# Sample states spread over forty branch products, head norms moved among the swish gate products

## What is computed

```python
u_x, u_y, q, k, v, g, mq, gates = split(rmsnorm(x) @ w_in)
a_out = (h * gelu(u_y)) @ w_branch_lru                 # recurrent branch
# retention, 4 heads; for a sample: s = s * decay + k v ; o = q s   (s0 from state_ret, s is an output)
o, s_new = retention(rotary(q), rotary(k), v, s_prev)
o = o * rsqrt(mean(o * o, per head) + EPS)             # head norm
b_out = (silu(g) * o) @ w_branch_ret                   # swish gate, then 2048 x 1024
c_out = attention(mq, mem_k, mem_v) @ w_branch_mem
merged = sigmoid(g_a) * a_out + sigmoid(g_b) * b_out + sigmoid(g_c) * c_out
x = x + merged @ w_out
x = x + moe(rmsnorm(x))                                # 32 experts of 3 x 2 MB, top 2 of a group
```

## Time and profile before

| | |
|---|---|
| median of 3 runs | 1172.71 us (1172.45 to 1174.39) |
| the profiled execution's own time | 1173.44 us |
| its span, first to last instruction | 1171.6 us |
| TensorE / its weight loads busy | 961.7 us (82%) / 705.9 us (60%) |
| VectorE / ScalarE / GpSimd busy | 366.6 / 221.4 / 100.9 us |
| granted TensorE clock, mean | 0.952 |
| moved by DMA | 343.8 MB, mean 293 GB/s |

### The profile page before, as it was taken

How to read it: one execution, slowest core, us unless ns; L and a number is a source line. 1 busy time by engine, 2 the same in 40 slices (tenths; PEclk the granted TensorE clock), 3 DMA queues, 4 the chain that set the end, 5 groups by cost and what they waited for, 6 DMA issues and landing times.

```text
span 1171.6 us, 16329 instructions
## 1 busy us (share of the span) xinstructions
PE 961.7 (82%) x6950; PEld 705.9 (60%) x6950; DVE 366.6 (31%) x681; ACT 221.4 (19%) x453; POOL 100.9 (9%) x122
## 2 busy tenths in 40 slices
PE   7999999999999888999999888566647667675655
PEld 6888888768876666788888645333324333333323
DVE  3303573376223224452111362111162111111113
ACT  2112124114331222241000142010101011010102
POOL 0001121000123332100000140000000000000000
PEclk9999999999999999999999999998988888889897
DMA  9874466694569799745347949999999999999991
GB/s 318 277 251 153 158 216 229 191 278 124 201 231 307 245 299 317 255 144 181 108 144 274 372 167 416 417 417 417 417 417 415 418 416 417 415 418 416 416 404 62
DMA packets 138825, 343.80 MB, mean 293 GB/s; under 512 B 7640, under 2 KB 91864, under 8 KB 122360
## 3 DMA queue, kind: packets, MB, share of 16 engines
q1 hardware_dynamic: 124288, 290.05, 65.7%
q0 software_dynamic: 14464, 52.68, 13.3%
HBM read 320.48 MB, written 22.20 MB: 292 GB/s over the span
## 4 chain that ended last, share of the span: by engine, by line
PE 47%; SPq 22%; DMA 20%; DVE 5%; issue 4%; ACT 2%; POOL 1%; DVEq 0%; ACTq 0%; POOLq 0%
PE psum L961 28%; SPq L783 22%; DMA out_ret_s<-arena 10%; DMA arena<-in_w_up 8%; PE psum L693 3%; PE psum L1015 3%; PE psum L970 2%; PE psum L1027 2%; PE psum L703 2%; PE psum L677 1%; ACT arena L1301 1%; DVE arena L1664 1%; DMA arena<-arena 1%; POOL arena L866 1%; DMA arena<-in_state_ret 1%
## 5 line engine op out<-in xcount | busy, mean ns | idle before, releaser
L961 PE MATMUL psum<-arena 128*128 128x264 f32 x2048 | 473.6, 388 | 0.0
L961 PEld LDWEIGHTS psum<-arena 128*128 128x128 f32 x2048 | 387.6, 191 | 76.3 <-issue 12.0
L693 PE MATMUL psum<-arena 128*32 128x256 f32 x2048 | 148.4, 440 | 119.0 <-DMA arena<-in_w_up 118.1
L693 PEld LDWEIGHTS psum<-arena 128*32 128x32 f32 x2048 | 79.0, 123 | 181.8 <-issue 158.0
L1301 ACT ACTIVATE arena<-psum 128x264 f32<-128x264 f32 (+5 forms) x160 | 67.5, 439 | 350.8 <-PE psum L961 269.0
L1965 DVE SCALAR_TENSOR_TENSOR arena<-arena,psum 128x128 f32<-128x128 f32 x32 | 9.2, 288 | 237.0 <-ACT arena L1510 237.0
L1301 ACT ACTIVATE arena<-arena 128x1024 f32<-128x1024 f32 (+7 forms) x67 | 58.7, 903 | 106.7 <-DVE arena L1819 84.8
L703 PE MATMUL psum<-arena 128*32 128x256 f32 x1024 | 66.4, 402 | 11.8 <-ACT arena L1522 11.7
L1772 DVE SCALAR_TENSOR_TENSOR arena<-arena 128x512 f32<-128x512 f32 x64 | 45.6, 774 | 82.0 <-ACT arena L1301 81.9
L1229 PE MATMUL psum<-arena 128*128 128x264 f32 x112 | 40.1, 441 | 24.1 <-DVE arena L1977 24.1
L703 PEld LDWEIGHTS psum<-arena 128*32 128x32 f32 x1024 | 31.2, 115 | 41.3 <-ACT arena L1522 21.9
(11 more groups left out here) (246 smaller groups left out, 738.1 us busy)
## 6 DMA issues: line engine op xcount, KB each, us to landing
arena<-in_w_gate SPq DMA_DIRECT2D x64, 1024.0 KB, 22.8
arena<-in_w_up SPq DMA_DIRECT2D x64, 1024.0 KB, 22.5
arena<-in_w_down SPq DMA_DIRECT2D x64, 1024.0 KB, 22.9
arena<-in_w_in SPq DMA_DIRECT2D x48, 1024.0 KB, 5.4
arena<-in_state_ret POOLq DMA_DIRECT2D x16, 1024.0 KB, 7.1
out_ret_s<-arena POOLq DMA_DIRECT2D x16, 1024.0 KB, 9.3
arena<-in_w_mem_kv SPq DMA_DIRECT2D x8, 1024.0 KB, 11.6
arena<-in_cache_mem_k POOLq DMA_DIRECT2D x8, 1024.0 KB, 5.6
```

The source lines that it names most:

```text
L693: mm = pe.matmul(psum[32 * a:32 * a + SLOTS, bank, 0:256], tokens[:, 4 * half + k, SLOTS * j:SLOTS * (j + 1)], w[:, :, k, P * a:P * (a + 1 ...
L961: mm = pe.matmul(ps(task)[:, 0:T], w[:, k, (i % 2) * P:(i % 2 + 1) * P], rhs[:, k, :], start=k == 0, stop=k == KT - 1 and not two)
```

## The change

The eight gb products join the branch products, so that the head products and the sixteen half states are woven over forty products instead of thirty-two. The head norms no longer stand among the gb products but among the first seven g products: soT directly behind gb7, oq0 before g0, oq1 and on0 before g1, oq2 and on1 before g2, oq3 and on2 before g4, on3 before g6. VectorE's part of a g task becomes a task of its own, ("gev", i), one g product later in the list, and it uses no PSUM bank of its own. The lifetimes of the buffers follow: what lived to "gc" now lives to "gb", and the norms' scratch lies in stage "g".

```diff
 BUFFERS = {
-    "dmask": (NMASK, "load", "gc"),
+    "dmask": (NMASK, "load", "gb"),
...
-    "st": (3 * 4 * DV, "rows", "gc"),
+    "st": (3 * 4 * DV, "rows", "gb"),
...
-    "os": (DV, "ga", "gb"),
+    "os": (DV, "ga", "g"),
...
-    "sq2": (2 * 4 * T, "gb", "gb"),
+    "sq2": (2 * 4 * T, "g", "g"),
...
-    branches = t("ga", 8) + t("lru_out", 8) + t("gc", 8) + t("mem_out", 8)
+    branches = t("ga", 8) + t("lru_out", 8) + t("gc", 8) + t("mem_out", 8) + t("gb", 8)
     middle = weave(branches, ret[1:])
-    onorm = [("soT",), ("oq", 0), ("oq", 1), ("on", 0), ("oq", 2), ("on", 1), ("oq", 3), ("on", 2), ("on", 3)]
+    norms = {0: [("oq", 0)], 1: [("oq", 1), ("on", 0)], 2: [("oq", 2), ("on", 1)], 4: [("oq", 3), ("on", 2)],
+             6: [("on", 3)]}
+    gated = [("soT",)]
+    for i in range(VT):
+        gated += norms.get(i, []) + [("g", i)] + ([("gev", i - 1)] if i else [])
+    gated += [("gev", VT - 1)]
...
-        + weave(t("gb", 8), onorm) + t("g", 16) + t("ret_out", 8) + t("x2", 8) + [("x2_sq",)]
+        + gated + t("ret_out", 8) + t("x2", 8) + [("x2_sq",)]
...
-                elif kind == "g":
+                elif kind == "gev":
                     i = task[1]
                     dve.wait_ge(g_tanh, i + 1)
                     x = gt[:, i % 2, :]
-                    v(V.scalar_tensor_tensor(x, x, 1.0, ps(task)[:, 0:T], ALU.add, ALU.mult), free_of(task))
+                    v(V.scalar_tensor_tensor(x, x, 1.0, ps(("g", i))[:, 0:T], ALU.add, ALU.mult), free_of(("g", i)))
                     v(V.tensor_tensor(oT[:, i, :], oT[:, i, :], x, ALU.mult), ret_ready)
```

More of the change, by code:

```diff
@@ L154 @@
     "conv_st": (KT * 16, "ux", "x2"),
-    "qT": (KT * T, "q", "gc"),
-    "kT": (KT * T, "k", "gc"),
+    "qT": (KT * T, "q", "gb"),
+    "kT": (KT * T, "k", "gb"),
     "rtmp": (HEADS * 2 * T, "k", "v"),
     "vT": (VT * T, "v", "rows"),
-    "vs_rows": (HEADS * DV, "rows", "gc"),
-    "vb": (2 * D, "rows", "gc"),
-    "st": (3 * 4 * DV, "rows", "gc"),
+    "vs_rows": (HEADS * DV, "rows", "gb"),
+    "vb": (2 * D, "rows", "gb"),
+    "st": (3 * 4 * DV, "rows", "gb"),
     "p32": (TP, "k", "k"),
@@ L164 @@
     "cs": (TP, "k", "rows"),
-    "QM": (KT * 2 * NS * NS, "k", "gc"),
+    "QM": (KT * 2 * NS * NS, "k", "gb"),
     "pqk": (KT * NS, "k", "rows"),
     "qkb": (HEADS * NS, "rows", "rows"),
-    "vqk": (VT * NS, "rows", "gb"),
-    "attT": (2 * 384, "rows", "gc"),
+    "vqk": (VT * NS, "rows", "g"),
+    "attT": (2 * 384, "rows", "gb"),
     "oT": (VT * T, "ga", "ret"),
-    "os": (DV, "ga", "gb"),
+    "os": (DV, "ga", "g"),
     "merged": (KT * T, "ga", "x2"),
@@ L306, in tensor_order @@
         + middle[:4] + weave(middle[4:], so)
-        + weave(t("gb", 8), onorm) + t("g", 16) + t("ret_out", 8) + t("x2", 8) + [("x2_sq",)]
+        + gated + t("ret_out", 8) + t("x2", 8) + [("x2_sq",)]
     )
-NO_PSUM = {"oq", "xq", "lam", "sd", "conv", "kl", "lru", "lru_root", "gelu", "gelu_tanh", "rot_q", "rot_k"}
+NO_PSUM = {"oq", "gev", "xq", "lam", "sd", "conv", "kl", "lru", "lru_root", "gelu", "gelu_tanh", "rot_q", "rot_k"}
 PROJECTIONS = {"mk", "mv", "mq", "ux", "uy", "q", "k", "v", "g", "ga", "gb", "gc", "lru_out", "ret_out",
```

## The result

The changed kernel takes 1165.4 us (median of 5, 1163.6 to 1166.75) against 1172.45 us (5 runs, 1171.4 to 1174.39): a ratio of 0.9938, 95% interval 0.9923 to 0.9952, so 7 us or 0.6% faster. The forecast was 1162.7 us, 10 us faster, with a range of 1152.5 to 1170.5. The sign, the mechanism and the range held; nearly a third of the forecast gain was missing.

What follows compares the result with a forecast made beforehand. Bound: neither TensorE nor DMA full in the state stage, then TensorE, then DMA. so15 at 485 + 11.5 work + 6.1 stall + 1.7 clock = g0 at 504.3 against 514.26, 10.0 us earlier: 1162.7 us, range 1152.5 to 1170.5.

Steps and rivals of the forecast that it cites:

- Where the gain is: State stage: forty products instead of thirty-two take up TensorE's waits for state loads, 17.4 us before the change.
- Part 1: State stage with forty products: the last state product, so15, starts at 485 us, wrong if after 490.
- The work term: State stage: TensorE's own work from first to last state product is 155.3 us, 10.35 us a state.
- The middle between TensorE's and DMA's pace: State stage: so15 at 480.6 us if TensorE is the bound, 489.7 at DMA's upper end; 485 taken.
- Part 2: Between so15 and the first gate product g0: 11.5 us of work remain, the head sums included.
- Part 3: Before the first head sum: TensorE stands still 6.1 us for the last state's decay, update, store, square and adds.
- The clock term: Behind the stall before the first head sum: one dip of TensorE's clock costs 1.7 us, between 0 and 3.4.
- The passing on: From g0 to the end: a shift of g0 passes on one for one, the expert stream included.
- A: First head sum: the sums find their data, no stall or clock dip; 17.8 us earlier, 1154.9 us; chance 0.15.
- B: State stage: weight chunks slow the states to 11.5 us each; 2.9 us later, 1175.6 us; chance 0.09.
- The norms among the gates: Behind the first head sum: heads and gates share ScalarE and VectorE without a second stall.
- The gates one place later: g products: evacuating the gates one place later costs nothing, as the room on ScalarE and VectorE hides it.

Runs made afterwards that it cites:

- e7: Changed kernel with each half state's store writing only the first quarter of its columns; 1157.4 us, ratio 0.989.
- e10: As e9, but in GpSimd's queue a half state's store goes before the load of the one two later; 1163.72 us, ratio 0.9938.
- e1: Changed kernel with the last decay and update directly behind the last head product, no longer behind gb6; 1161.26 us, ratio 0.9917.
- e2: Changed kernel with the first head sum one g product later, other sums and gate evacuations moved later accordingly; 1162.55 us, ratio 0.9932.
- e11: The changed kernel measured again unaltered, beside the kernel before on one chip; 1164.33 against 1171.81 us, ratio 0.9935.
- e9: As e3, but the second head sum stands behind two more gate evacuations on VectorE; 1156.97 us, ratio 0.9881.
- e4: Kernel before with only the norms moved among the g products, states still woven over thirty-two products; 1171.34 us, ratio 0.9998.
- e3: Changed kernel with both the moves of e1 and e2; 1159.82 us, ratio 0.9903.

## Why the prediction was right, and where it was too large

- *Where the gain is.* Right. Waits for state loads fell from 17.4 to 4.7 us, and with the stores cut to a quarter the gain is gone.
- *Part 1, so15 at 485.* Right within 1.8 us in the first trace (486.83) and on the mark in the second (484.98). The work term, 155.3 us, measured 154.1 in e7. The middle between TensorE's and DMA's pace was a choice that nothing in the rows fixed, and that it came so close is partly luck: in the six traces with forty products, whole stores and the old queue order the stage is 4.7 to 8.3 us above those 154.1, in e10 12.8.
- *Part 2, 11.5 us of other work.* Right: 9.7 us from so15 to g0 (496.50), and 1.8 for the four head sums.
- *Part 3, the stand.* Right in place, cause and size: square at so15 + 16.7 (forecast 16.8), first sum at + 19.1 (19.3), TensorE there at + 13.5 (13.4), stand 5.6 (6.1; the two forecast marks by themselves give 5.9). e1 took 3.7 us from it, e2 3.5.
- *The clock term is the one that was mis-sized.* I priced one dip, 5 us at a granted clock of 0.66 behind a wait of 1.95 us, so 1.7 us, and had two of them, 3.4, as the other end. The trace of the kernel before shows what one costs; that a stand of 6 us costs one was my estimate. Behind a stand of 5.6 us the head sum and g1 took 1.25 and 6.17 us where 0.61 and 3.72 are usual: 3.1 us, at a granted clock of 0.51, then 0.81 (505 to 510, 510 to 515 us). In the second execution (e11) it was 1.6, close to the price, at 0.86, then 0.80 (500 to 505, 505 to 510 us).
- *The sum.* 486.8 + 11.5 + 5.6 + 3.1 = 507.0 against 504.3: the 10.0 us become 7.3, and ret_out's second half indeed starts 7.1 us earlier (567.71 against 574.78, TensorE's timeline). Of the missing 2.7 us the late so15 has 1.8 and the clock 1.4, less 0.5 of the stand; both lie within what differs between executions. In the second execution every term came within 0.5 us of the forecast (so15 at 484.98, stand 5.7, clock 1.6), and it took 1163.71 us where 1163.4 was forecast for the profiled one. That the medians beside it still differ by only 7.5 us lies at the ends: the one trace of the kernel before from which all was counted took 1173.44 us, 1.6 above the median beside e11 (the forecast took off 0.7), and e11's trace lies 0.6 below its own median.
- *The passing on.* Right: the gather ahead of the first expert starts 6.75 us earlier (686.29 for 693.04), and from there to the end it is 477.3 us for 478.6.
- *Rivals.* A (no stand) did not come, but e9 shows that, with the last decay and the head sums moved, most of it was there to be had: 17.8 us forecast, 13.7 measured. B's price of 11.5 us a state did not come with forty (160.8 / 15 = 10.7); the stage's growth with every product put in points the way of B at less than its price, and no run separates what the chunks have in it.
- *Costed at nothing.* The norms among the gates: right (e4). The gates one place later: right in the changed kernel. That "four banks" leave room was too easy a sentence, though: with the sums one product later, one misplaced on1 cost 2.1 us and a clock dip (e3).

## What to carry to other kernels

Work moved under a stage that waits for DMA is worth the waits it fills, not its own length, and the stage grows by part of it: here 25 us of products, with their weight chunks, moved in lengthened it by 10 and filled 13 us of waits, and the other 2 us are clock no longer lost (0.98 for 0.95 in the longer part). Ask in the same breath which chain hangs on the stage's last item and what covered it; here three places in the lists (the last decay, the first head sum with those behind it, and the second head sum) were together worth nearly as much again as the change itself (e9). Of the way of the last state to the first sum the longest part is the 5.8 us of its store, which the first square waits for only because it may lie on the state buffers; no run gave the squares a place of their own. When an expectation rests on one profile, compare marks inside the trace rather than spans: from the gather to the end the twelve profiled executions took 477.3 to 481.0 us, a spread of half the effect, with nothing changed there.

## What the runs showed of the hardware

The length of a stand did not set what the clock took behind it. Taken from products that ran longer than usual, it was nothing after 1.9 us (e1, granted clock 1.00), 1.8 us after 2.1 (e3, 0.80, then 0.86 in the windows of 5 us from 515 us), 1.7 after 2.2 (e2, 0.98, then 0.68 from 500 us), 1.8 after 4.1 (e7, 0.80, then 0.86 from 495 us), and 3.1 and 1.6 us after 5.6 and 5.7 in two executions of the same kernel (0.51, then 0.81 from 505 us; 0.86, then 0.80 from 500 us); the wait of 2.0 us in the kernel before cost 1.7 by the clock of one window, 0.66. And a store of a quarter of the bytes reached the engine waiting for it only 1.5 us sooner (4.33 for 5.80 us), with a weight chunk beside it both times (DMA share 0.73 and 0.88).
